# First feed-forward in parts of 8, 8 and 6 hidden tiles with six groups of gate and up pairs as seven block products, its state tables built behind them

## The chip, the cores and the metric

The kernel runs on one core of one Trainium2 chip. Times are device microseconds of that core. The engines are PE (TensorE: products), DVE (VectorE) and ACT (ScalarE) for work by element, POOL (GpSimd), and SP, which issues most of the transfers.

## What is computed

Two decoder layers over 528 tokens (16 meta tokens and 512) of 1024 features, in float32. The feed-forward has 2816 hidden features, 22 tiles of 128.

```python
def swiglu(x, w_gate, w_up, w_down):
    return (jax.nn.silu(x @ w_gate) * (x @ w_up)) @ w_down

def hybrid_layer(x, ...):
    x = layer_norm(ALPHA * x + 0.5 * swiglu(x, ffn1_w_gate, ffn1_w_up, ffn1_w_down), ln1_g, ln1_b)
    proj = x @ w_in
    ...                                   # three mixers: attention, short convolution, S5 scan
    x = layer_norm(ALPHA * x + mixed @ w_o, ln2_g, ln2_b)
    x = layer_norm(ALPHA * x + 0.5 * swiglu(x, ffn2_w_gate, ffn2_w_up, ffn2_w_down), ln3_g, ln3_b)
    return x
```

The S5 mixer needs tables made of its parameters alone: powers of its complex transition applied to the input weights (s_in_states, here in_step), to the output weights (s_out, here out_step), the powers themselves by token group (s_turns, here turn_step), and short kernels made of two of them (s_kernels).

## The kernel before

**Products.** Every product is made in three passes over parts that TensorE takes in its fast float32 form: high part of the weights by high part of the inputs, high by low, low by high (`product`). The 528 tokens are two halves of 264 columns, so a chunk of weights (8 tiles of 128x128) makes 48 products. A chunk is loaded by SP into one of two raw buffers (`load`), rounded to w_hi by ACT (`round_ahead`, `round_at`, line 1348), its remainder w_lo is made by POOL (`split`, line 642), and it lies in a ring of four slots until PE is done with it. PE, ACT, DVE and POOL each run an order written out by hand, and wait for each other on semaphores.

**Feed-forward.** The hidden tiles are made in three parts (PARTS: 6, 8, 8 tiles). In a part each tile needs a gate product and an up product; ACT takes the silu of the gate (hid_rest), DVE multiplies (line 1956) and splits the result (lines 1957 and 1958). Behind a part stand eight down products, one for each tile of 128 output features, which DVE takes into ln_in (line 1977; line 2108 in the second feed-forward). The down products of the last part are made in halves from the fifth on (`last_tiles`, line 840) so that the layer norm can begin on the first half; DVE takes them at line 1861 and goes on with the statistics (`tail`), and the products behind the norm (`first_products`, line 753 and 730) run over the first half of the tokens first.

**Crossed groups.** In the second feed-forward a pair of gate tiles, or of up tiles, is a 2x2 block product: the features in two halves, the tokens in two halves. It is made as seven products of blocks instead of eight (`crossed`, line 864). It needs turned inputs, that is four sums and differences of the blocks of x (DVE lines 1994 to 1997), rounded by ACT (turned_hi) with remainders by DVE (line 2002), made once per feed-forward; four sums of weight blocks per unit (`add_weights`, line 2018); and five additions of the results (`combine`, line 2036). The weights are loaded as pairs (w_pair). In most units ACT first copies three weight blocks into PSUM banks (`copy_block`), and the sums read them there. A crossed unit's seven forms (half chunks of 512 columns) are rounded and split one by one; form 5 waits for the second addition. In part 0 the second feed-forward has one plain pair and two pairs with only the gate crossed, in parts 1 and 2 gate and up are crossed.

**First feed-forward.** All its pairs are plain, and POOL, ACT, PE and SP run them in loops. DVE makes the state's tables beside them (`tables_beside`): angles, turn, coefficients beside the first three tiles; in_step beside part 0's later tiles and part 1's; out_step beside part 1's; turn steps 0 to 5 beside part 0's down products, 6 and 7 in part 1. PE transposes the tables beside part 1's down products (`turn_inputs`), and makes the kernels before part 2 (`s5_kernels`); ACT takes them (`take_turned`, `take_kernels`). Behind the layer norm come the mixer's first ten projections (`m1`), in which PE makes the states (line 1025) that DVE takes in `scan_begin` (line 2290).

## Time and profile before

| | us |
| --- | --- |
| median of 3 runs | 2550.42 (2549.15 to 2551.89) |
| the profiled execution | 2552.9 |
| its span | 2551.1 |
| PE busy in the span | 2509.9 |
| DVE busy | 1382.7 |
| ACT busy | 951.4 |
| POOL busy | 1230.0 |

The profile is one execution. Its page gives for each engine the busy time, a slice view, the chain of work that ended last, and the costliest groups of instructions. In a row of a timeline stand the start and the length in us, engine, line, operation, what it writes and reads, the number of instructions that the row merges, and in brackets how long the engine was idle before and what ended that. Layer 0's first feed-forward is from 10 to 406 us, its second from 918 to 1284; layer 1's first is from 1287 to 1682.

### The profile page before, as it was taken

To read this page: it belongs to the slowest core of one execution; us is meant where nothing else is said; L and a number is where in the kernel's file an instruction comes from. 1 tells how busy PE (TensorE), PEld (TensorE's weight loads), DVE (VectorE), ACT (ScalarE), POOL (GpSimd) and SP (SyncE) were. 2 spreads that over 40 slices of the span, in tenths; PEclk is the share of its full clock that TensorE was granted. 3 is DMA by queue.
4 is the path that set the end of the run, shared out by engine and by line. 5 is a ranking of instruction groups with operands and counts; after the bars stand their busy time and mean duration, and the time that the engine had idled before them with its cause. 6 is when DMAs were issued, how large, how long until landed. Compare 5 with 4: busy or idle time off the path is not lost.

```text
span 2551.1 us, 50807 instructions
## 1 busy us (share of the span) xinstructions
PE 2509.9 (98%) x20068; PEld 2391.4 (94%) x20068; DVE 1382.7 (54%) x2456; ACT 951.4 (37%) x1670; POOL 1230.0 (48%) x710
## 2 busy tenths in 40 slices
PE   9999999999999999999999999999999999999997
PEld 9999999998899999999999999999977788989897
DVE  6683134784453484535566841347844535835366
ACT  4222223235532243636452222232355322537363
POOL 4443344523234456867554443445332454668582
PEclk9999999999999999999999999999999999999999
DMA  5333233432223333333333323334322333324232
GB/s 154 93 91 90 84 91 84 111 82 65 60 79 89 95 92 100 91 108 89 95 93 99 90 83 91 91 83 110 84 65 63 87 88 106 100 83 117 83 102 81
DMA packets 479725, 232.25 MB, mean 91 GB/s; under 512 B 58960, under 2 KB 479056, under 8 KB 479536
## 3 DMA queue, kind: packets, MB, share of 16 engines
q1 hardware_dynamic: 460288, 220.53, 31.9%
q10 hardware_dynamic: 19248, 9.08, 1.5%
q8 instruction: 133, 2.18, 0.4%
q14 instruction: 56, 0.46, 0.1%
HBM read 220.79 MB, written 4.26 MB: 88 GB/s over the span
## 4 chain that ended last, share of the span: by engine, by line
PE 91%; DVE 4%; issue 3%; POOL 1%; ACT 1%; DMA 0%; ACTq 0%; POOLq 0%; DVEq 0%; SPq 0%
PE ps L730 64%; PE ps L864 14%; PE ps L840 4%; PE ps L753 3%; PE ps L1177 1%; PE ps L1216 1%; POOL w_lo L642 1%; PE ps L1181 1%; PE ps L1192 1%; DVE ln_in L1916 0%; PE ps L1099 0%; ACT ln_in L1348 0%; DVE ps L1933 0%; PE ps L1089 0%; PE ps L799 0%
## 5 line engine op out<-in xcount | busy, mean ns | idle before, releaser
L642 POOL TENSOR_TENSOR w_lo<-w_raw,w_hi 128x1024 fp32r<-128x1024 f32 (+4 forms) x400 | 850.5, 2133 | 1100.6 <-ACT w_hi L1348 1099.9
L1348 ACT ACTIVATE w_hi<-w_raw 128x1024 fp32r<-128x1024 f32 (+4 forms) x400 | 373.0, 936 | 659.3 <-PE ps L730 381.5
L730 PE MATMUL ps<-x_hi,w_hi 128*128 128x264 f32 (+2 forms) x2720 | 398.4, 296 | 2.5 <-issue 1.3
L730 PE MATMUL ps<-x_hi,w_lo 128*128 128x264 f32 (+2 forms) x2720 | 389.2, 293 | 0.6 <-POOL w_lo L642 0.6
L730 PE MATMUL ps<-x_lo,w_hi 128*128 128x264 f32 (+2 forms) x2720 | 389.0, 293 | 0.0
L730 PEld LDWEIGHTS ps<-x_hi,w_hi 128*128 128x128 f32 x2720 | 356.7, 189 | 16.7 <-issue 2.2
L730 PEld LDWEIGHTS ps<-x_hi,w_lo 128*128 128x128 f32 x2720 | 355.3, 188 | 11.0 <-POOL w_lo L642 1.3
L730 PEld LDWEIGHTS ps<-x_lo,w_hi 128*128 128x128 f32 x2720 | 355.4, 188 | 9.8
L1956 DVE TENSOR_TENSOR ps<-hid_rest,ps 128x528 f32<-128x528 f32 (+1 forms) x56 | 39.7, 710 | 242.8 <-PE ps L730 230.1
L730 PE MATMUL ps<-hid_hi,w_hi 128*128 128x264 f32 (+1 forms) x1008 | 158.2, 301 | 0.1
L730 PE MATMUL ps<-hid_hi,w_lo 128*128 128x264 f32 (+1 forms) x1008 | 156.6, 299 | 0.0
L642 POOL TENSOR_TENSOR w_lo<-w_sum,w_hi 128x512 fp32r<-128x512 f32 x90 | 118.7, 1325 | 78.3 <-ACT w_hi L1348 77.8
L730 PE MATMUL ps<-hid_lo,w_hi 128*128 128x264 f32 (+1 forms) x1008 | 156.4, 299 | 0.0
L642 POOL TENSOR_TENSOR w_lo<-w_pair,w_hi 128x512 fp32r<-128x512 f32 x108 | 145.1, 1358 | 9.7 <-ACT w_hi L1348 9.7
L730 PEld LDWEIGHTS ps<-hid_hi,w_hi 128*128 128x128 f32 x1008 | 137.1, 188 | 6.7 <-DVE ln_in L1977 0.6
L730 PEld LDWEIGHTS ps<-hid_hi,w_lo 128*128 128x128 f32 x1008 | 137.2, 188 | 6.3
L730 PEld LDWEIGHTS ps<-hid_lo,w_hi 128*128 128x128 f32 x1008 | 137.0, 188 | 6.2
L1348 ACT ACTIVATE hid_rest<-ps 128x528 f32 (+2 forms) x88 | 51.1, 603 | 173.9 <-PE ps L730 158.9
L2461 DVE SCALAR_TENSOR_TENSOR stat<-stat,ps 128x528 f32<-128x528 f32 (+1 forms) x32 | 22.2, 695 | 158.0 <-PE ps L730 158.0
L1348 ACT ACTIVATE w_hi<-w_sum 128x512 fp32r<-128x512 f32 x90 | 56.4, 631 | 101.6 <-DVE w_sum L2018 66.8
L864 PE MATMUL ps<-turned_lo,w_hi 128*128 128x264 f32 (+1 forms) x576 | 92.6, 283 | 0.0
L864 PE MATMUL ps<-turned_hi,w_hi 128*128 128x264 f32 (+1 forms) x576 | 92.5, 282 | 0.0
(349 smaller groups left out, 4303.3 us busy)
## 6 DMA issues: line engine op xcount, KB each, us to landing
w_raw<-in_w_in SPq DMA_DIRECT2D x82, 512.0 KB, 3.9
w_raw<-in_ffn_w_down SPq DMA_DIRECT2D x64, 512.0 KB, 3.9
w_raw<-in_ffn_w_up SPq DMA_DIRECT2D x56, 512.0 KB, 3.8
w_raw<-in_ffn_w_gate SPq DMA_DIRECT2D x48, 512.0 KB, 3.8
w_pair<-in_ffn_w_gate SPq DMA_DIRECT2D x40, 512.0 KB, 5.1
w_pair<-in_ffn_w_up SPq DMA_DIRECT2D x32, 512.0 KB, 5.2
w_raw<-in_ffn_w_down SPq DMA_DIRECT2D x32, 384.0 KB, 3.4
w_raw<-in_w_o SPq DMA_DIRECT2D x16, 512.0 KB, 3.9
```

Of the source, the lines that this page charges most:

```text
L642: pool.tensor_tensor(held(w_lo, c), src, held(w_hi, c).bitcast(f32), ALU.subtract).then_inc(w_split, 1)
L730: ins = nc.tensor.matmul(dst, wk, x[:, k0 + k, tokens], start=first and k == 0 and n == 0, stop=last and k == n_tiles - 1 and n == 2)
L753: ins = nc.tensor.matmul(dst, held(w, c + j, k * P, (k + 1) * P), x[:, k, tokens], start=k == 0 and n == 0, stop=k == nk - 1 and n == 2)
L840: ins = nc.tensor.matmul(ps[:, bank, 0:sp.half], held(w, c + d, k * P, (k + 1) * P), x[:, k, sp.halves[h]], start=p == 0 and k == 0, stop= ...
L864: ins = nc.tensor.matmul(ps[:, banks + bank, 0:sp.half], held(w, c + n, k * P, (k + 1) * P), x[:, k], start=start and i == 0 and k == 0, s ...
L1177: ins = nc.tensor.matmul(ps[0:nq, j % 2, 0:q0 + nq], qT[:, b, q0:q0 + nq], kT[:, b, 0:q0 + nq], start=True, stop=True)
L1181: ins = nc.tensor.matmul(ps[0:nq, h, 0:HALF], qT[:, b, q0:q0 + nq], kT[:, b, h * HALF:(h + 1) * HALF], start=True, stop=True)
L1192: nc.tensor.transpose(ps[:, 2 + buf, k * P:(k + 1) * P], pr[:, buf, k * P:(k + 1) * P], ident[:])
L1216: ins = nc.tensor.matmul(ps[64 * part:64 * part + 64, o_bank(i, b, part), q0 - first:end - first], vb[0:nk, b, k, :], PT[0:nk, k, q0:end], ...
L1348: return nc.scalar.activation(out, in_, f, **kw)
L1956: st.done(tt(up, gate, up, MUL))
L2461: ins = stt(two(stat[:, 2, sp.all]), two(stat[:, n % 2, sp.all]), 1.0, pair(2 * (n % 2) + 1, sp), ADD, MUL)
```

## The change

The first feed-forward gets parts of 8, 8 and 6 hidden tiles. Pairs 0 and 1 of part 0 stay plain; pairs 2 and 3 of part 0 and all four pairs of part 1 become crossed groups, gate and up, by the code of the second feed-forward, which is made general for both (w is 0 or 1). The three pairs of part 2 stay plain. There are 30 units per layer for 18. The turned inputs of the first feed-forward are made from ln_in at its start. Four of its forms skip half a slot of the ring.

The space of the turned inputs, of the weight pairs and of their sums is that of the tables. So in_step goes to the down products of part 1, behind a wait for the last unit's splits; out_step goes to the tiles of part 2; the turn steps go behind the layer norm, ahead of `scan_begin`. The load of s_out goes behind the third down product of part 1, on ACT's queue. PE's transposes go into pairs 1 and 2 of part 2, the kernels into the last tile of part 2 (banks 0 and 1), and PE waits for ACT's copies of them ahead of the down products. s_params moves by one row. The loops of the first feed-forward are written out. The second feed-forward stays as it is.

```diff
-TURN_WITH = [(0,), (1,), (2,), (3,), (4,), (5,), (6, 7), ()]
+TURN_BANK = [0, 1, 0, 1, 4, 5, 4, 5]
+OUT_STEPS = [(1, 2), (3, 4), (5, 6), (7,), (), ()]
+TAKE_WITH = {(0, 0): (), (0, 1): (), (1, 0): (0, 1), (1, 1): (2, 3, 4, 5), (2, 0): (6, 7), (2, 1): ()}
-PARTS = [(0, 6), (6, 8), (14, 8)]
+PARTS_OF = [[(0, 8), (8, 8), (16, 6)], [(0, 6), (6, 8), (14, 8)]]
+LAST = 2
+FIRST_CROSSED = 2
...
+def crossed_in(w, part, q):
+
+    if w:
+        return () if (part, q) == (0, 0) else (0, 1) if part else (0,)
+    return () if part == LAST or (part == 0 and q < FIRST_CROSSED) else (0, 1)
...
+BESIDE = [n for n, (w, part, q, what) in enumerate(UNITS)
+          if len(crossed_in(w, part, q)) == 2 and (what or (w, part, q - 1, 1) in UNITS)]
+SKIP_HALF = [UNIT_AT[0, 1, q, what] + 3 for q in (0, 2) for what in range(2)]
...
@@ SP
+            def load_pair(l, n):
+
+                w, part, q, what = UNITS[n]
...
+                if n in (FFN2_UNIT, FFN2_UNIT + 1):
+                    wait_apart(sp, chunk_done, done_at(l, B_WO + KD - 1))
+                elif g >= 2:
+                    wait_apart(sp, w_split, unit_split(g - 2))
...
+                            if part == 0 and crossed_in(w, part, q + 1):
+                                load_pair(l, UNITS.index((w, part, q + 1, 0)))
...
+                        for what in whats:
+                            n = UNITS.index((w, part, q, what))
+                            if n + 1 < N_CROSS and UNITS[n + 1][0] == w:
+                                load_pair(l, n + 1)
...
@@ PE
+            def regular_group(l, part, q, n0, t0, turned):
+
+                for j in range(2):
+                    c = GROUPS_AT[0, part, q] + 2 * j
+                    rounded(l, c)
+                    pe.wait_ge(silu_done, n0 + q * 2 + (j + 1))
+                    if turned and q == 2:
+                        pe.wait_ge(lf_taken, l * 8 + (4, 8)[j])
+                    product(pair(2 * j), c, 0, xh, xl, KD, True, True, split=(l, c)).then_inc(chunk_done, 1)
+                    if turned and (q, j) == (1, 1):
+                        turn_inputs(l, 2)
+                        turn_inputs(l, 3)
+                    if turned and (q, j) == (2, 0):
+                        turn_inputs(l, 6)
+                        turn_inputs(l, 7)
+                    if turned and (q, j) == (2, 1):
+                        pe.wait_ge(silu_done, n0 + (2 * q + 3))
+                        s5_kernels(l)
+                    rounded(l, c + 1)
+                    if part:
                         pe.wait_ge(z_taken, t0 + 2)
...
+                    if turned and q == 1:
+                        pe.wait_ge(silu_done, n0 + (2 * q + j + 3))
+                        turn_inputs(l, 4 * j)
+                        turn_inputs(l, 4 * j + 1)
...
                     pe.wait_ge(silu_done, n0 + (nf + 1))
+                    if w == 0 and part == LAST:
+                        pe.wait_ge(k_taken, l * 4 + 4)
...
@@ ACT
+                def first_group():
+
+                    c = GROUPS_AT[w, 0, 0]
...
+                    act.wait_ge(chunk_done, done_at(l, c))
+                    silu(0, pair(0, sp), 1.0)
+                    round_at(l, c + 1)
+                    if w == 0:
+                        act.wait_ge(s5p_in, l * 16 + 16)
+                        ACTV(s5p[:, 2], s5p[:, 2], ACT.Exp).then_inc(dt_done, 1)
+                    act.wait_ge(chunk_done, done_at(l, c + 2))
+                    silu(1, pair(2, sp), 1.0)
+                    round_at(l, c + 2)
+                    if w == 0:
+                        act.wait_ge(trig_in, l + 1)
+                        ACTV(s5p[:, 3], s5p[:, 3], ACT.Exp)
+                        ACTV(s5p[:, 6], s5p[:, 4], ACT.Sin)
+                        ACTV(s5p[:, 7], s5p[:, 4], ACT.Sin, scale=0.5).then_inc(trig_done, 1)
+                        act.wait_ge(par_in, l * 16 + 16)
+                        round_turned(0)
+                        round_turned(1)
+                    round_turned(2)
+                    round_turned(3)
+                    round_at(l, c + 3)
...
+                            if w == 0 and part == 1 and d == 2:
+                                wait_apart(act, w_split, unit_split(l * N_CROSS + FFN2_UNIT - 1))
...
+                                    act.dma_start(cl[r, :, :, 0].rearrange("p k q h -> p (k q) h"),
...
@@ DVE
+                def first_groups():
+
+                    c = GROUPS_AT[w, 0, 0]
+                    turn_inputs()
...
+                    s5_angles(l, st)
+                    hidden(0, 0, c + 1, 1)
+                    hidden(0, 1, c + 3, 3)
+                    s5_turn(l, st)
+                    for k in range(4):
+                        turned_rest(k)
+                    add_weights(0)
+                    hidden(0, 2, c + 5, 1)
+                    s5_coefficients(l, st)
+                    hidden(0, 3, c + 7, 3)
+
+                def regular_group(part, q):
+
+                    for j in range(2):
+                        hidden(part, 2 * q + j, GROUPS_AT[0, part, q] + (2 * j + 1), 2 * j + 1)
+                        for k in OUT_STEPS[2 * q + j]:
+                            out_step(l, k, st)
+                        if 2 * q + j == PARTS_OF[0][part][1] - 2:
+                            layer_norm_shift(sp)
...
                     for d in range(KD):
                         dve.wait_ge(chunk_done, done_at(l, bd + d))
                         ins = stt(two(z[:, d, sp.all]), pair(d % 2, sp), 0.5 / ALPHA, two(z[:, d, sp.all]), MUL, ADD)
                         follow(ins, z_taken, t0 + (d + 3))
+                        if w == 0 and part == 1:
+                            if d == 0:
+                                dve.wait_ge(w_split, unit_split(l * N_CROSS + FFN2_UNIT - 1))
+                            in_step(l, d, st)
...
-                ffn(l, B_FFN1, 0, st)
+                ffn(l, 0, st)
+                for d in range(8):
+                    turn_step(l, d, st)
                 scan_begin(l, st)
```

## Rows read from the trace of the kernel before

**Rows 1.** The page: engines; chain that ended last; costliest groups (busy, mean ns, idle).
```profile
PE 2509.9 (98%) x20068; PEld 2391.4 (94%) x20068; DVE 1382.7 (54%) x2456; ACT 951.4 (37%) x1670; POOL 1230.0 (48%) x710
...
PE 91%; DVE 4%; issue 3%; POOL 1%; ACT 1%; DMA 0%; ACTq 0%; POOLq 0%; DVEq 0%; SPq 0%
...
L1956 DVE TENSOR_TENSOR ps<-hid_rest,ps 128x528 f32<-128x528 f32 (+1 forms) x56 | 39.7, 710 | 242.8 <-PE ps L730 230.1
```

**Rows 2.** Stretches: length, busy of PE, PEld, DVE, ACT, POOL, clock, DMA.
```profile
146.88:170.08 23.20, 23.20 (x194) 23.20 (x194) 22.57 (x32) 5.24 (x7) 9.89 (x4) 1.00 0.31 89
...
1056.81:1077.20 20.39, 20.39 (x170) 20.39 (x170) 12.49 (x22) 14.16 (x28) 17.69 (x15) 1.00 0.38 105
```

**Rows 3.** Timelines at the start, layer 0 then layer 1; last ACT's turned_hi (min/median/max).
```profile
36.08 2.09 PE L730 MATMUL ps<-x_hi,w_hi 128*128 128x264 f32 x16
...
37.47 0.17 DVE L2140 TENSOR_SCALAR s_params<-s_params 128x16 f32<-128x16 f32 x1
...
1313.74 2.09 PE L730 MATMUL ps<-x_hi,w_hi 128*128 128x264 f32 x16
...
1317.87 0.17 DVE L2140 TENSOR_SCALAR s_params<-s_params 128x16 f32<-128x16 f32 x1
...
1319.61 1.28 ACT L1348 ACT_TABLE_LOAD   x1
...
1324.05 1.06 ACT L1348 ACTIVATE w_hi<-w_raw 128x1024 fp32r<-128x1024 f32 x1
...
L1348 ACT ACTIVATE turned_hi<-turned_raw x8: 1044/1067/1087, 939.6 to 2209.8; 128x1056 fp32r<-128x1056 f32 x4, 128x1024 fp32r<-128x1024 f32 x4
```

**Rows 4.** DVE, second feed-forward, layer 0: timeline of its entry; groups of one later group.
```profile
943.90 1.26 DVE L2002 SCALAR_TENSOR_TENSOR turned_lo<-turned_raw,turned_hi 128x1056 fp32r<-128x1056 f32 x1
...
945.80 2.78 DVE L2018 TENSOR_TENSOR w_sum<-w_sum,w_pair 128x512 f32<-128x512 f32 x1
...
956.82 2.24 DVE L2002 SCALAR_TENSOR_TENSOR turned_lo<-turned_raw,turned_hi 128x1056 fp32r<-128x1056 f32 x1
...
L2036 DVE TENSOR_TENSOR ps<-crossed_sum,ps 128x264 f32<-128x264 f32 x6 | 2.6, 437 | 2.5 <-PE ps L864 2.4
L2018 DVE TENSOR_TENSOR w_sum<-w_pair,ps 128x512 f32<-128x512 f32 x3 | 2.1, 686 | 2.8 <-ACT ps L1348 2.8
```

**Rows 5.** Timelines of POOL and DVE, layer 1, first feed-forward.
```profile
1312.09 4.88 POOL L642 TENSOR_TENSOR w_lo<-w_raw,w_hi 128x1024 fp32r<-128x1024 f32 x2 [5.33 <-ACT w_hi L1348]
...
1314.63 2.36 DVE L2136 TENSOR_SCALAR s_params<-s_params 128x16 f32<-128x16 f32 x1
```

**Rows 6.** POOL by shape, 947.95 to 961.45, entry of layer 0's second feed-forward.
```profile
L642 POOL TENSOR_TENSOR w_lo<-w_pair,w_hi 128x512 fp32r<-128x512 f32 x3 | 6.3, 2117 | 0.0
L642 POOL TENSOR_TENSOR w_lo<-w_sum,w_hi 128x512 fp32r<-128x512 f32 x4 | 5.9, 1484 | 1.4 <-ACT w_hi L1348 1.4
```

**Rows 7.** DVE's takes of down products of a part with 8 tiles.
```profile
1142.08 0.71 DVE L2108 SCALAR_TENSOR_TENSOR ln_in<-ps,ln_in 128x528 f32<-128x528 f32 x1 [5.11 <-PE ps L730]
1147.88 0.71 DVE L2108 SCALAR_TENSOR_TENSOR ln_in<-ps,ln_in 128x528 f32<-128x528 f32 x1 [5.09 <-PE ps L730]
```

**Rows 8.** PE behind the last part of layer 0's first feed-forward.
```profile
407.94 0.36 PE L753 MATMUL ps<-x_hi,w_hi 128*128 128x264 f32 x1 [1.84 <-DVE ln_in L1861]
```

**Rows 9.** DVE's tables: in_step's and out_step's rows; stretches of one in_step, the first.
```profile
166.40 1.93 DVE L2193 TENSOR_TENSOR s_tmp<-s_lambda,s_in_states 128x256 f32<-128x256 f32 x1
...
171.32 3.63 DVE L2244 TENSOR_TENSOR s_tmp<-s_lambda,s_out 128x256 f32<-128x256 f32 x4
...
166.48:171.29 4.81, 4.81 (x42) 4.81 (x41) 4.77 (x7) 1.21 (x2) 1.33 (x1) 1.00 0.38 109
61.77:68.81 7.04, 7.04 (x60) 7.04 (x59) 6.93 (x12) 2.98 (x4) 2.92 (x2) 1.00 0.19 56
```

**Rows 10.** Sum of three stretches with the turn steps; DVE's next work behind the norm.
```profile
sum 29.82, PE 29.82 PEld 29.82 DVE 26.00 ACT 7.37 POOL 12.98; mean PE 9.94 PEld 9.94 DVE 8.67 ACT 2.46 POOL 4.33
...
458.59 0.43 DVE L2290 TENSOR_TENSOR s_state<-ps,s_turns_re 128x260 f32<-128x260 f32 x1 [30.73 <-PE ps L1025]
```

More of the change, by code:

```diff
@@ L680, in _ @@
             for l in range(DEPTH):
-                ffn(l, B_FFN1)
+                for c in range(B_FFN1 + SLOTS, B_M1):
+                    split(l, c)
                 norm(l, 0, B_M1)
@@ new lines, in regular_group @@
+                def regular_group(part, q):
+                    for j in range(2):
+                        c = GROUPS_AT[0, part, q] + 2 * j
+                        round_at(l, c)
+                        act.wait_ge(chunk_done, done_at(l, c))
+                        silu(2 * q + j, pair(2 * j), 1.0)
+                        round_at(l, c + 1)
+                        if part == LAST:
+                            for n in TAKE_WITH[q, j]:
+                                take_turned(l, n)
+                    if part == LAST and q == 2:
+                        take_kernels(l)
```

472 lines of the change are left out of this document (184 added, 288 removed).

## Prediction

> **What bounds the kernel now.** I read the views in this order. The page [rows 1]: PE is busy for 98% of the span, and 91% of the chain that ended last is PE. So a change is worth the PE time that it takes away, less what it makes PE wait. Then the table of stretches [rows 2]: a group of the first feed-forward (two gate and two up tiles, 528 tokens) lasts 23.20 us with PE busy in all of it; a crossed group of the second feed-forward of layer 0, over the same 528 tokens, lasts 20.39 us and PE is busy in all of that too. That is 168 products for 192 at the same 0.121 us each, at a granted clock of 1.00. Then the timelines of each engine at the places where something moves: they give durations, and which wait ends last.
>
> **The groups that become products of blocks.** Twelve change, six per layer: pairs 2 and 3 of part 0 and the four of part 1. Each replaces 23.2 us by 20.4 [rows 2]: 12 x 2.8 = 33.6 us less. ACT, DVE and POOL must keep up; in the second feed-forward they do, busy for 14.2, 12.5 and 17.7 us of 20.4 [rows 2]. Spans, block copies and order are the same in the first, and its tables are built elsewhere, so nothing is added beside these groups. The new split into parts costs PE nothing by itself: 22 hidden tiles times 8 outputs either way.
>
> **Entry: the turned inputs,** new in the first feed-forward of both layers. I price two waits, by the rows of layer 1 [rows 3].
> ACT first. It now rounds the four turned inputs (1.07 us each) before the weights of gate tile 3. The angles are ready at 1318.0; three table loads with the exponential and the sines took 4.4 us (1319.6 to 1324.0), so they end at 1322.5, the roundings at 1326.8, the weight chunk (1.06) at 1327.8. PE starts pair 1 at 1313.7 and wants the chunk 11.6 us later, at 1325.3: it waits 2.5 us. In layer 0 the angles are ready 1.6 us after the start of pair 1 instead of 4.3: chunk at 47.4, wanted at 47.7, no wait.
> DVE next. From the angles on it does hidden tiles 0 and 1 (2 x 3 instructions of 0.71 [rows 1]), the turn (some 17 of 0.16), four remainders of turned inputs (1.26), four sums of weights (0.69), hidden 2, the coefficients (some 20 of 0.16) and hidden 3 [rows 3 to 5]: 4.3 + 2.7 + 5.0 + 2.8 + 2.1 + 3.2 + 2.1 = 22.2 us, to 1340.3. At the entry of the second feed-forward, 943.90 to 959.06, the same remainders and sums with one hidden tile took 15.2 us for 10.0 unhindered, because single instructions were drawn out to 2.24 and 2.78 us [rows 4]. Those 5.2 us make it 1345.5. ACT's copy of a weight block waits for hidden 3, whose bank it takes, and behind it on ACT stand the roundings of forms 5 and 6; copy, one sum (0.69) and two combinations (0.43 each) add 2.2 us [rows 4]: 1347.7. PE, 2.5 us late, wants form 5 at 1346.7. So 1.0 us is lost; unhindered nothing is, with twice the hindrance 6.2. I take 2.0, near the low end, since its row is of the same instructions. In layer 0 both sides lie 2.5 to 2.7 us earlier: 2.0 again. Entry: 2.5 + 2.0 + 2.0 = 6.5 us, bounds 2.5 and 14.9.
> What draws DVE out is to be seen in [rows 5]: a tiny instruction lasts 2.36 us and ends with the POOL splits that ran from 1312.09 to 1316.97. The Trainium skill ("SBUF — State Buffer", section "SBUF: two separate sides") says that VectorE and GpSimd take a shared pair of ports as an exclusive lock, for instance for a VectorE instruction with two SBUF inputs. By that rule the remainders and sums hold up POOL as well, which speaks against this change; the trace agrees, as the seven forms of that entry took 12.2 us [rows 6].
>
> **Exit: a shorter last part.** It falls from 8 to 6 hidden tiles, so less PE work lies beside the layer norm: a down product takes 4.35 us for 5.80 [rows 7], a half 2.2 for 2.9. Before, PE waits 1.84 us for a DVE take (L1861) ahead of the mixer's first products [rows 8]. After the first half's sums three halves are left to PE, 2.1 us shorter in future, while DVE's chain to that take shrinks by 0.7 only, a wait for one of the halves. So the gap becomes some 3.2 to 3.4 us: +1.6 a layer, 3.2 in all, bounds 0 and 4.4 (no part of 2.2 hidden).
>
> **The state's tables, moved.** In_step goes beside the down products of part 1. One took 4.8 us, of which its first instruction 1.93; the first, with two complex products, 6.9 [rows 9]. With the take (0.71) the cycle is 5.5 us for a product of 5.80 [rows 7]. The first runs over by 1.9, but PE asks only for the take of two products earlier: 3.3 us of slack remain, nothing is lost. Out_steps take at most 4.5 us [rows 9]; two and a hidden tile are 11.1 of the 11.6 us of a tile, and the table is ready some 10 us before the kernels' products ask. Transposes and kernels' products stay PE work, the same number, between other products; ACT's copies of the kernels lie beside the last up product. The load of s_out moves to ACT's queue behind the third down product of part 1, with over 30 us to land, and ACT is mostly idle there. On SP pair loads stand ahead of down weights and wait for the split of two units back, as in the second feed-forward. The Toeplitz copies wait for the kernels some 90 us longer and still lie ahead of the end of the mixer's projections.
> The turn steps go behind the layer norm: the stretches with them hold 26.0 us of DVE work, less five takes of 0.71: 22.5 us. DVE is idle for 30.73 us ahead of 458.59, where PE's states come [rows 10]: hidden, 8 us to spare; without that cover 22.5 us per layer.
>
> **The rivals.** (1) *The edges cost nothing beyond ACT's wait*: -33.6 + 2.5 = -31.1. For it: the second feed-forward's entry has the drawn-out instructions and no PE gap. Against: one hidden tile there, no tables. (2) *The tables push the down products.* If a second hindrance of 1.3 us (1.93 against some 0.65) falls into each in_step, the cycle is 6.8 us; 8 x 1.0 less the slack of 3.3 is 4.7 us per layer: -23.9 + 9.4 = -14.5. With three it is 8 x 2.3 - 3.3 = 15.1 per layer: +6, no gain. For it: POOL splits beside these products; against: one split per 5.8 us, as beside the gates, where [rows 9] shows one hindrance. (3) *POOL sets the pace, and it is slower than before.* A group then lasts 14 splits; the seven at the entry of the second feed-forward took 1.75 us each [rows 6], which makes 24.5 us: 12 x (24.5 - 23.2) + 9.7 = +25 us. It decides at 23.2 / 14 = 1.66 us a split (1.60 with the edges). For it: POOL has but 2.7 us spare; against: 17.7 / 14 = 1.26 us in settled groups [rows 2]. The skill's lock is this mechanism; by that rule alone a group lies between 20.4 and 24.5 us. (4) *It doesn't do what it says*: groups are crossed but PE runs slower in unrolled code or waits for pair loads. At 21.5 us a group it is 12 x 1.7 = 20.4 less and 9.7 more: -10.7. Against: the crossed groups are unrolled already, without a gap [rows 2].
>
> **How the numbers follow.** Forecast: -33.6 + 6.5 + 3.2 = -23.9 us. The profiled execution took 2552.9 us (span 2551.1 and 1.8 around it), so 2529.0. The median of the runs is 2550.4, 2.5 lower: 2526.5 us. Chances: forecast 0.55 (2521 to 2532), free edges 0.20 (2519.3), late tables 0.14 (2536, of which 0.04 reach 2545 or more), POOL's pace 0.05 (2575), slower products 0.06 (2540). The bounds give -33.6 + 2.5 + 0 = -31.1 and -33.6 + 14.9 + 4.4 = -14.3: 2519.3 to 2536.1; I reach down to 2517, since ACT's wait may be absent too. 0.2%, 5.1 us, is about what a measurement of this kernel can tell from no change. Faster by more: 0.90; within: 0.05; slower: 0.05.
>
> **What would show it.** Silus of the first feed-forward some 20.4 us apart over six groups per layer and 23.2 over the others; PE gaps of 1 to 3 us at the first crossed group and at gate tile 3 of layer 1, ended by ACT roundings; some 3.3 us for 1.84 behind the last part; takes 5.8 us apart in part 1; turn steps ended before the states. It is wrong if POOL's splits take over 1.5 us in settled groups, if down products of part 1 lie over 6 us apart, or if PE waits for turn steps or a pair's load.

## The result, and the profile after

The changed kernel takes 2534.49 us (median of five runs, 2532.34 to 2539.03) against 2550.93 us of five runs of the kernel before beside them: a ratio of 0.9941, 95% interval 0.9929 to 0.9952, so 16.4 us less. The profiled execution took 2532.34 us with a span of 2530.5, the lowest of the five; its span is 20.6 us under that of the kernel before. A second set of five runs gave 2535.63 us (ratio 0.9937, 0.9923 to 0.9951), and its profile a span of 2533.8.

Line numbers have moved: products are L746, the first tiles behind a norm L769, crossed products L881, all of ACT's work L1376, POOL's splits L667, DVE's takes of down products L2136, its takes of halves L1879, and the six instructions of a complex product L2209 to L2216.

The page of the changed kernel, its line of engines and its chain that ended last (they answer to [rows 1]):

```profile
PE 2482.1 (98%) x19780; PEld 2361.1 (93%) x19780; DVE 1520.0 (60%) x2664; ACT 1047.4 (41%) x1900; POOL 1347.1 (53%) x830
...
PE 88%; DVE 5%; issue 4%; ACT 1%; POOL 1%; DMA 1%; ACTq 0%; POOLq 0%; SPq 0%; DVEq 0%
```

PE is busy 27.8 us less, with 288 products fewer, and the part of the chain that isn't PE has grown from 9% to 12%. So some of what was taken away came back as waits. Stretches (columns as in [rows 2]): a crossed group of part 1, two tiles of part 2, and the first step of in_step.

```profile
180.49:200.86 20.37, 20.37 (x170) 20.37 (x170) 12.49 (x22) 13.65 (x26) 17.58 (x15) 1.00 0.38 103
285.83:309.81 23.98, 23.48 (x194) 23.51 (x195) 21.90 (x33) 5.25 (x7) 10.08 (x4) 1.00 0.29 82
237.35:246.60 9.25, 9.25 (x78) 9.25 (x78) 9.11 (x13) 2.12 (x2) 5.02 (x3) 1.00 0.64 151
```

A crossed group lasts 20.37 us with PE busy in all of it: the gain is there, in full. Three places give some of it back. First, the entry. PE at the first crossed unit of layer 1, and then of layer 0:

```profile
1329.93 0.64 PE L881 MATMUL ps<-x_hi,w_lo 128*128 128x264 f32 x4
1333.88 1.06 PE L881 MATMUL ps<-turned_hi,w_hi 128*128 128x264 f32 x4 [3.31 <-issue]
1334.73 1.08 PE L881 MATMUL ps<-turned_lo,w_hi 128*128 128x264 f32 x4
...
1337.92 0.65 PE L881 MATMUL ps<-x_hi,w_lo 128*128 128x264 f32 x4
...
68.47 0.73 PE L881 MATMUL ps<-turned_hi,w_hi 128*128 128x264 f32 x4 [1.95 <-issue]
```

and DVE beside the first of them:

```profile
1309.88 6.82 DVE L2001 SCALAR_TENSOR_TENSOR turned_lo<-turned_raw,turned_hi 128x1056 fp32r<-128x1056 f32 x2
...
1322.83 1.32 DVE L2182 TENSOR_TENSOR s_params<-s_turn 128x16 f32<-128x16 f32 x1
...
1325.37 1.28 DVE L2186 TENSOR_TENSOR s_params<-s_params 128x16 f32<-128x16 f32 x1
...
1329.14 0.71 DVE L1974 TENSOR_TENSOR ps<-hid_rest,ps 128x528 f32<-128x528 f32 x1
...
1332.17 0.69 DVE L2017 TENSOR_TENSOR w_sum<-w_pair,ps 128x512 f32<-128x512 f32 x1 [0.83 <-ACT ps L1376]
1332.89 0.43 DVE L2035 TENSOR_TENSOR crossed_sum<-crossed_first,ps 128x264 f32<-128x264 f32 x1
1333.35 0.43 DVE L2035 TENSOR_TENSOR crossed_sum<-crossed_sum,ps 128x264 f32<-128x264 f32 x1
```

PE has made forms 0 to 4 of the unit (the row of 1329.93 ends form 4) and goes on at 1333.88, 0.10 us after the second addition (1333.35 + 0.43): form 5 waits for it. Layer 0 has one more gap there, of 0.38 us (77.82). "issue" names no releaser; the row of DVE does. The addition stands behind hidden tile 3 (from 1329.14), and that behind the coefficients, 1322.6 to 1329.1.

Second, beside part 1's down products. DVE, then POOL, then PE, in layer 1:

```profile
1531.99 0.71 DVE L2136 SCALAR_TENSOR_TENSOR ln_in<-ps,ln_in 128x528 f32<-128x528 f32 x1
...
1534.43 0.67 DVE L2212 TENSOR_TENSOR s_tmp<-s_lambda,s_in_states 128x256 f32<-128x256 f32 x1
1535.14 2.75 DVE L2215 TENSOR_TENSOR s_in_states<-s_tmp 128x256 f32<-128x256 f32 x1
1537.71 0.68 DVE L2216 TENSOR_TENSOR s_in_states<-s_tmp 128x256 f32<-128x256 f32 x1
1538.43 0.71 DVE L2136 SCALAR_TENSOR_TENSOR ln_in<-ps,ln_in 128x528 f32<-128x528 f32 x1
...
1533.63 3.74 POOL L667 TENSOR_TENSOR w_lo<-w_raw,w_hi 128x1024 fp32r<-128x1024 f32 x1 [2.68 <-ACT w_hi L1376]
...
1539.19 2.22 PE L746 MATMUL ps<-hid_hi,w_hi 128*128 128x264 f32 x16 [0.37 <-DVE ln_in L2136]
```

Takes lie 6.44 us apart (1531.99 to 1538.43) for a down product of 5.80 [rows 7], DVE has no idle time, and PE waits for the take. Of an in_step's six instructions one lasts 2.75 us and ends 0.52 us behind the split (1537.89 for 1533.63 + 3.74 = 1537.37), so it got its own 0.66 us of work done about when the split was over. PE has five such gaps in layer 0 (0.31, 0.32, 0.41, 0.39, 0.54 us) and four in layer 1 (0.30, 0.37, 0.43, 0.45).

Third, the exit, behind the first feed-forward of layer 0 (they answer to [rows 8]):

```profile
394.39 0.36 PE L769 MATMUL ps<-x_hi,w_hi 128*128 128x264 f32 x1 [1.13 <-DVE ln_in L1879]
...
397.42 0.36 PE L769 MATMUL ps<-x_hi,w_hi 128*128 128x264 f32 x1 [2.43 <-DVE ln_in L1879]
```

3.56 us for 1.84; layer 1 has 1.13 + 2.52. The two profiles differ also where the change does nothing, here to the good of the changed kernel: PE in the state's outputs, before and after.

```profile
537.72 0.56 PE L1099 MATMUL ps<-s_state,s_out 64*64 64x66 f32 x19 [1.87 <-issue]
```

```profile
523.23 0.57 PE L1127 MATMUL ps<-s_state,s_out 64*64 64x66 f32 x20 [0.40 <-issue]
```

Layer 0 of the kernel before also waited 1.30 us ahead of part 2 (264.65), beside ACT's copies of the kernels (from 262.87), which the change moved; layer 1 had no such gap.

### The profile page after: what moved, and what is told of

The parts are those of the page before. It is cut to its first block, busy times and chain, and to the rows that moved or that the text cites. A ratio compares the mean times of both kernels' runs of the same rounds, so it can differ in the third digit from the quotient of the medians.

```text
span 2530.5 us, 50304 instructions
## 1 busy us (share of the span) xinstructions
PE 2482.1 (98%) x19780; PEld 2361.1 (93%) x19780; DVE 1520.0 (60%) x2664; ACT 1047.4 (41%) x1900; POOL 1347.1 (53%) x830
## 4 chain that ended last, share of the span: by engine, by line
PE 88%; DVE 5%; issue 4%; ACT 1%; POOL 1%; DMA 1%; ACTq 0%; POOLq 0%; SPq 0%; DVEq 0%
PE ps L746 52%; PE ps L881 23%; PE ps L856 3%; PE ps L769 3%; PE ps L1205 1%; PE ps L1244 1%; POOL w_lo L667 1%; PE ps L1209 1%; PE ps L1220 1%; DVE s_in_states L2216 0%; ACT ln_in L1376 0%; DMA w_pair<-in_ffn_w_gate 0%; ACT x_hi L1376 0%; DVE ln_in L2136 0%; DVE s_tmp L2209 0%
## 5 line engine op out<-in xcount | busy, mean ns | idle before, releaser
L667 POOL TENSOR_TENSOR w_lo<-w_raw,w_hi 128x1024 fp32r<-128x1024 f32 (+3 forms) x352 | 753.1, 2149 | 895.6 <-ACT w_hi L1376 895.5
L1376 ACT ACTIVATE w_hi<-w_raw 128x1024 fp32r<-128x1024 f32 (+3 forms) x352 | 319.6, 913 | 589.2 <-PE ps L746 249.3
L746 PE MATMUL ps<-x_hi,w_hi 128*128 128x264 f32 (+2 forms) x1952 | 297.0, 301 | 2.2 <-issue 1.0
L746 PE MATMUL ps<-x_hi,w_lo 128*128 128x264 f32 (+2 forms) x1952 | 288.5, 297 | 0.6 <-POOL w_lo L667 0.6
L746 PE MATMUL ps<-x_lo,w_hi 128*128 128x264 f32 (+2 forms) x1952 | 288.4, 297 | 0.0
L746 PEld LDWEIGHTS ps<-x_hi,w_hi 128*128 128x128 f32 x1952 | 259.1, 188 | 16.9 <-issue 1.8
L746 PEld LDWEIGHTS ps<-x_hi,w_lo 128*128 128x128 f32 x1952 | 259.3, 188 | 11.1 <-POOL w_lo L667 1.3
L667 POOL TENSOR_TENSOR w_lo<-w_sum,w_hi 128x512 fp32r<-128x512 f32 x150 | 197.1, 1321 | 135.6 <-ACT w_hi L1376 134.8
L746 PEld LDWEIGHTS ps<-x_lo,w_hi 128*128 128x128 f32 x1952 | 259.4, 188 | 9.7
L667 POOL TENSOR_TENSOR w_lo<-w_pair,w_hi 128x512 fp32r<-128x512 f32 x180 | 238.7, 1341 | 23.6 <-ACT w_hi L1376 23.6
L746 PE MATMUL ps<-hid_hi,w_hi 128*128 128x264 f32 (+1 forms) x1040 | 162.3, 300 | 1.8 <-DVE ln_in L2136 1.7
L1376 ACT ACTIVATE w_hi<-w_sum 128x512 fp32r<-128x512 f32 x150 | 93.9, 630 | 166.6 <-DVE w_sum L2017 101.5
L746 PE MATMUL ps<-hid_hi,w_lo 128*128 128x264 f32 (+1 forms) x1040 | 161.1, 299 | 0.0
L746 PE MATMUL ps<-hid_lo,w_hi 128*128 128x264 f32 (+1 forms) x1040 | 161.0, 299 | 0.0
L881 PE MATMUL ps<-turned_hi,w_hi 128*128 128x264 f32 (+1 forms) x960 | 155.0, 283 | 5.3 <-issue 5.3
L2136 DVE SCALAR_TENSOR_TENSOR ln_in<-ps,ln_in 128x528 f32<-128x528 f32 (+1 forms) x64 | 45.0, 703 | 186.3 <-PE ps L746 185.7
L881 PE MATMUL ps<-turned_lo,w_hi 128*128 128x264 f32 (+1 forms) x960 | 155.3, 284 | 0.0
L881 PE MATMUL ps<-turned_hi,w_lo 128*128 128x264 f32 (+1 forms) x960 | 154.6, 283 | 0.0
L746 PEld LDWEIGHTS ps<-hid_hi,w_hi 128*128 128x128 f32 x1040 | 141.4, 188 | 9.7 <-DVE ln_in L2136 2.3
L746 PEld LDWEIGHTS ps<-hid_hi,w_lo 128*128 128x128 f32 x1040 | 141.3, 188 | 6.3
L746 PEld LDWEIGHTS ps<-hid_lo,w_hi 128*128 128x128 f32 x1040 | 141.1, 188 | 6.2
L881 PEld LDWEIGHTS ps<-turned_hi,w_hi 128*128 128x128 f32 x960 | 132.1, 188 | 6.4 <-issue 5.6
```

The costliest lines, as they stand in the source:

```text
L667: pool.tensor_tensor(held(w_lo, c), src, held(w_hi, c).bitcast(f32), ALU.subtract).then_inc(w_split, 1)
L746: ins = nc.tensor.matmul(dst, wk, x[:, k0 + k, tokens], start=first and k == 0 and n == 0, stop=last and k == n_tiles - 1 and n == 2)
L881: ins = nc.tensor.matmul(ps[:, banks + bank, 0:sp.half], held(wx, c + n, k * P, (k + 1) * P), x[:, k], start=start and i == 0 and k == 0, ...
L1376: return nc.scalar.activation(out, in_, f, **kw)
L2136: ins = stt(two(z[:, d, sp.all]), pair(d % 2, sp), 0.5 / ALPHA, two(z[:, d, sp.all]), MUL, ADD)
```

## The experiments

All medians stand against the kernel before run on the same chip, which gave 2549.9 to 2550.9 us. The changed kernel is 2534.5 and 2535.6 in its two sets.

**1. The coefficients out of the entry.** Nothing of the first feed-forward needs them.

```diff
                     hidden(0, 2, c + 5, 1)
-                    s5_coefficients(l, st)
                     hidden(0, 3, c + 7, 3)
...
                         follow(ins, z_taken, t0 + (d + 3))
+                        if (w, part, d) == (0, 0, 0):
+                            s5_coefficients(l, st)
```

> The changed kernel with the coefficients of the state (some 20 small instructions on DVE, 6.5 us in the trace of the changed kernel, 1322.6 to 1329.1) taken out from between hidden tiles 2 and 3 and put beside the first down product of part 0, where DVE is mostly idle. Theory A (DVE's chain hidden 3, block copy, sum, two additions ends PE's wait ahead of form 5): hidden 3 ends 6.5 us earlier, so the gaps of 1.95 us (layer 0) and 3.31 us (layer 1) go, and with them the slow stretch behind the second (four rows of 1.06 us for 0.65, 1.6 us): 6.8 us less, 2534.5 - 6.8 = 2527.7 us (2525.5 to 2530). Rival B (PE waits for forms whose roundings or splits are late, whatever DVE does): the gaps stay within 0.5 us, 2534 us. Rival C (the drawn-out remainders in front are what counts and a new wait for DVE's sums takes the place of the old one): half goes, 2531.

Measured: 2527.45 us (2525.43 to 2530.52), ratio 0.9914 (0.9900 to 0.9927). The gaps of 1.95, 0.38 and 3.31 us are gone, and the slow stretch too. DVE and then PE at the same place in layer 1:

```profile
1320.36 0.71 DVE L1976 TENSOR_TENSOR hid_lo<-ps,hid_hi 128x528 fp32r<-128x528 f32 x1
1322.71 0.69 DVE L2017 TENSOR_TENSOR w_sum<-w_pair,ps 128x512 f32<-128x512 f32 x1 [1.64 <-ACT ps L1376]
1323.43 0.43 DVE L2035 TENSOR_TENSOR crossed_sum<-crossed_first,ps 128x264 f32<-128x264 f32 x1
1324.67 0.43 DVE L2035 TENSOR_TENSOR crossed_sum<-crossed_sum,ps 128x264 f32<-128x264 f32 x1 [0.81 <-PE ps L881]
...
1325.38 0.64 PE L881 MATMUL ps<-x_hi,w_lo 128*128 128x264 f32 x4
1325.86 0.65 PE L881 MATMUL ps<-turned_hi,w_hi 128*128 128x264 f32 x4
```

Now DVE waits for PE ahead of the second addition (0.81 us), not PE for DVE. Theory A holds for the gaps, B and C fall. But the 7.0 us are not the entry alone. From the silu ahead of it to the last one of part 0 layer 0 is 2.85 and layer 1 5.05 us shorter, 7.9 in all. Beside part 0's down products, where the coefficients now stand, the two layers lose 0.8 us (a gap of 0.36 us at 117.95). And beside part 1's down products, which this edit doesn't touch, layer 0 lost nothing any more (2.75 us less than in the changed kernel), while layer 1 lost about what it had lost before. DVE and POOL there, layer 0:

```profile
247.97 0.71 DVE L2135 SCALAR_TENSOR_TENSOR ln_in<-ps,ln_in 128x528 f32<-128x528 f32 x1
248.71 2.01 DVE L2210 TENSOR_TENSOR s_tmp<-s_lambda,s_in_states 128x256 f32<-128x256 f32 x1
...
247.81 2.40 POOL L667 TENSOR_TENSOR w_lo<-w_raw,w_hi 128x1024 fp32r<-128x1024 f32 x1 [3.32 <-ACT w_hi L1376]
```

Here the split starts ahead of the take and is over 1.5 us after in_step's first instruction began. That instruction is drawn out by 1.35 us, the split by nothing, and the takes lie 5.56 to 5.87 us apart. The first step took 7.03 us. So the same in_step beside the same products has two courses, and this one is that of the prediction.

**2. in_step spread.** A pause beside the third down product, the last step behind the first hidden tile of part 2, out_steps one tile later.

```diff
-OUT_STEPS = [(1, 2), (3, 4), (5, 6), (7,), (), ()]
+OUT_STEPS = [(), (1, 2), (3, 4), (5, 6), (7,), ()]
+IN_STEPS = [(0,), (1,), (), (2,), (3,), (4,), (5,), (6,)]
...
+                        if (q, j) == (0, 0):
+                            in_step(l, 7, st)
...
-                            in_step(l, d, st)
+                            for k in IN_STEPS[d]:
+                                in_step(l, k, st)
```

> The changed kernel with in_step's eight steps spread otherwise: none beside the third down product of part 1, the last one behind the first hidden tile of part 2, and the out_steps one tile later each. Theory A (DVE's cycle of take and in_step, 6.45 us in the trace against a down product of 5.80, holds up the products): DVE catches up once in the middle, and the gaps ahead of the later down products (0.31 + 0.32 + 0.41 + 0.39 + 0.54 us in layer 0, 0.30 + 0.37 + 0.43 + 0.45 in layer 1, with 0.1 us of slower first products each) go: 3.5 to 4.4 us less, 2534.5 - 4 = 2530.5 us (2529 to 2532). Rival B (the gaps come with each down product for another reason, such as the slower splits of 3.9 us): they stay, 2534.5. Rival C (the out_steps, one tile later, are late for the kernels' products): PE waits there, 2536 or more.

Measured: 2529.76 us (2528.54 to 2531.01), ratio 0.9918 (0.9904 to 0.9932), 4.7 us under the changed kernel. Of the nine gaps two are left, ahead of the fourth down product, one in each layer:

```profile
254.43 1.69 PE L747 MATMUL ps<-hid_hi,w_hi 128*128 128x264 f32 x12 [0.33 <-DVE ln_in L2139]
...
1519.62 1.69 PE L747 MATMUL ps<-hid_hi,w_hi 128*128 128x264 f32 x12 [0.65 <-DVE ln_in L2139]
```

They are the debt of the first step, two complex products that took 9.25 us beside a product of 5.80. The pause does more than give slack: behind it the steps run as in layer 0 of experiment 1 (in layer 0 from 268.17 on the first instruction takes 2.05 to 2.22 us, and the splits 2.40). The out_steps, a tile later, were in time.

**3. Splits made thin.** What draws in_step out. The low parts of part 1's down weights are left out but for 8 of 1024 columns.

```diff
+                n = 8 if DOWN_AT[0][1] <= c < DOWN_AT[0][1] + KD else COLS[c % CH]
-                pool.tensor_tensor(held(w_lo, c), src, held(w_hi, c).bitcast(f32), ALU.subtract).then_inc(w_split, 1)
+                pool.tensor_tensor(held(w_lo, c, 0, n), src[:, 0:n], held(w_hi, c, 0, n).bitcast(f32),
+                                   ALU.subtract).then_inc(w_split, 1)
```

> The changed kernel with POOL's splits of part 1's down weights made over 8 of 1024 columns: the low parts of these weights are left out. Theory A (one instruction of each in_step is drawn out from 0.66 to 2.75 us because POOL's split holds it up): every instruction of in_step lasts some 0.66, the cycle of take and in_step is 6.45 - 2.1 = 4.35 us, takes lie 5.80 us apart and PE has no gap over 0.2 us beside these products; some 4 us less than the changed kernel, profiled 2528. Rival B (DVE's sixth instruction is long by its own addresses, s_in_states written with a stride): it stays 2.75 us and the gaps of 0.3 to 0.5 stay.

Measured in one execution: 2529.62 us. DVE and POOL in layer 0:

```profile
249.38 0.41 POOL L668 TENSOR_TENSOR w_lo<-w_raw,w_hi 128x8 fp32r<-128x8 f32 x1 [5.39 <-ACT w_hi L1378]
...
250.78 0.65 DVE L2214 TENSOR_TENSOR s_tmp<-s_lambda,s_in_states 128x256 f32<-128x256 f32 x1
251.47 0.66 DVE L2217 TENSOR_TENSOR s_in_states<-s_tmp 128x256 f32<-128x256 f32 x1
254.11 0.71 DVE L2138 SCALAR_TENSOR_TENSOR ln_in<-ps,ln_in 128x528 f32<-128x528 f32 x1 [1.48 <-PE ps L748]
```

The instruction of 2.75 us lasts 0.66, take and in_step together 4.32 us, DVE waits 1.48 us for PE in each cycle, and PE has no gap beside these products. From the last silu ahead of them to the first behind they take 61.34 us in both layers, for 64.09 and 63.62 in the changed kernel: 5.0 us in all are the price of the split's hold on DVE, as the two met in the changed kernel. Theory A holds. (Layer 0 of experiment 1 took 61.3 us too, with whole splits.)

**4. Part 0 plain.** Only the four groups of part 1 crossed.

```diff
-FIRST_CROSSED = 2
+FIRST_CROSSED = 4
...
-SKIP_HALF = [UNIT_AT[0, 1, q, what] + 3 for q in (0, 2) for what in range(2)]
+SKIP_HALF = []
...
```

The lines left out let DVE make hidden tiles 4 to 7 plain and move the load of the first pair of weights.

> The changed kernel with all of part 0 of the first feed-forward plain again; only the four pairs of part 1 are crossed (eight groups in all, for twelve). The turned inputs are still made at the start. By 2.8 us a group the four plain groups cost 11.2 us. Theory A (the entry's losses come only from crossing at once behind the first pairs: gaps of 1.95 and 0.38 in layer 0, of 3.31 and 0.37 in layer 1 and 1.6 us of slow clock): they go, 7.2 to 7.6 us come back, 2534.5 + 11.2 - 7.4 = 2538.3 us (2536.5 to 2540.5). Rival B (they come from making the turned inputs at the start, whoever uses them): they stay, 2545.7. Rival C (a crossed group of part 0 is worth less than 2.8 us): below 2535.

Measured: 2544.31 us (nine runs, 2541.02 to 2547.60), ratio 0.9976 (0.9966 to 0.9986). It is 6.0 us from A's number and 1.4 from B's, but the trace decides for A: no gap stands where the four were, though the turned inputs are made at the same place, so B falls. And a group is worth what it should be; a plain one of part 0 and a crossed one of part 1 in this kernel:

```profile
65.31:88.51 23.20, 23.20 (x194) 23.20 (x193) 8.13 (x19) 5.36 (x6) 10.28 (x5) 1.00 0.36 101
184.44:204.81 20.37, 20.37 (x170) 20.37 (x169) 12.50 (x22) 14.14 (x27) 17.68 (x15) 1.00 0.38 104
```

Of the 6 us over A's time 2.0 are found beside part 1's down products, where the same in_step met the splits at other moments (silu to silu 65.29 and 64.37 us for 64.09 and 63.62; its first step took 10.3 us, with instructions of 1.68, 2.50 and 2.75). The rest lies in stages that this edit doesn't touch, 1.6 us of it in one longer gap ahead of layer 1's second feed-forward; why it is longer was not found.

**5. Two edits together.** Experiments 1 and 2, with the pause one product earlier (`IN_STEPS = [(0,), (), (1,), (2,), (3,), (4,), (5,), (6,)]`), to pay the first step's debt where it arises.

> The two edits that paid, together: the state's coefficients beside the first down product of part 0, and in_step's steps with a pause beside the second down product of part 1 (one down product earlier than in the run before, because the first step took 9.3 us for two complex products and left a gap of 0.33 and 0.65 us at the fourth), the eighth behind the first hidden tile of part 2. Theory A (two separate waits, so the gains add): 7.0 + 4.7 us off 2534.5, and 1 us for the two gaps: 2521.8 us (2520 to 2524.5). Rival B (they share slack: what PE doesn't wait at the entry it waits for at the down products): 2525 or more.

Measured: 2521.62 us (2519.99 to 2523.14), ratio 0.9888 (0.9873 to 0.9903). The gains add, so B falls by its number. They are not two wholly separate waits, though: in layer 0 experiment 1 alone had already taken the loss beside part 1's down products. With both edits it is gone in both layers (61.3 us from silu to silu in either), and beside part 0's down products, with the coefficients, PE loses 1.1 and 0.7 us in the second set's profile. That set (expected as follows) gave 2521.31 us.

> The kernel with both edits again, beside the one with the takes in the other order: 2521.6 us (2520 to 2523).

**6. The exit: is it the shorter part?** Each half of the last four down products multiplies two of its six hidden tiles a second time, so that PE takes a part of 8's time there.

```diff
-                            for k in range(nk):
+                            order = [*range(nk), *((0, 1) if which == 0 else ())]
+                            for i, k in enumerate(order):
...
```

> The changed kernel in which each output half of the last four down products of the first feed-forward multiplies two of its six hidden tiles a second time, so that PE takes the time of a part of 8 tiles there (8 halves x 6 products x 0.121 us = 5.8 us more work a layer); what is computed differs in that. Theory A (the gap behind the first feed-forward went from 1.84 to 3.56 us because the shorter last part leaves PE less to do beside DVE's layer norm): the gap falls to about 1.8 us in each layer; 2535 + 11.6 - 3.5 = 2543 us. Rival B (the gap grew for another reason, such as DVE's tail being later by the tables): it stays 3.5 us, 2547 us.

Measured in one execution: 2541.60 us. The same row as in the changed kernel, layer 0 and layer 1:

```profile
402.55 0.36 PE L769 MATMUL ps<-x_hi,w_hi 128*128 128x264 f32 x1 [1.82 <-DVE ln_in L1880]
...
1672.77 0.36 PE L769 MATMUL ps<-x_hi,w_hi 128*128 128x264 f32 x1 [1.83 <-DVE ln_in L1880]
```

The gap is back at the 1.84 us of [rows 8]: DVE's tail is as long as it was, and PE had 5.8 us less to do beside it, of which 1.7 show as a wait. Theory A holds.

**7. DVE's last two takes together.** At every layer norm, on top of experiment 5; and once on the changed kernel alone.

```diff
-                        if h == 0 and k in (2, 3):
-                            st.done(add_half_square(k + 3, 1, k + 8))
-                            take_half(k + 4, 1)
+                        if h == 0 and k == 2:
+                            st.done(add_half_square(5, 1, 10))
+                            take_half(6, 1)
+                            take_half(7, 1)
+                        if h == 0 and k == 3:
+                            st.done(add_half_square(6, 1, 11))
```

> The run before, and at every layer norm DVE takes the last two output halves of the second half one right behind the other. In the trace PE has long made the last half (393.25) when DVE takes it at 396.84, behind a square, a scaling and a remainder, and PE's second column of the next products waits for its bank: gaps of 1.13 + 2.43 us behind the first feed-forward (1.84 before the change), 1.83, 2.79 and 1.93 behind the others. Theory A (the order of DVE's takes sets the gap): PE starts 2.4 us earlier and waits later for tiles of x, of which DVE makes one in 1.5 us where PE uses 0.7: 0.5 to 1.5 us less at each of five norms, some 4 us, 2518 us. Rival B (DVE's whole tail is the bound, the order changes nothing): the gaps split up and their sum stays, within 1.5 us of the run before. Rival C: the tiles of x come 0.9 us later for the two takes ahead of them, and each norm loses that: 4 us more.

> Only the order of DVE's takes at the layer norms changed, all else as the changed kernel: a look at where PE then waits. Theory A: one gap of about 1.1 us for the bank, then small ones of 0.3 to 1 us for tiles of x, 2.5 us in sum for 3.56 behind the first feed-forward; 2530.5 us. Rival B: the sum of the gaps stays 3.5 us, 2534 us. Rival C: over 4 us in sum, 2538.

> The kernel with both edits and DVE's takes in the other order again. In the look at the changed kernel with this order the gaps behind the first feed-forward were 2.3 us for 3.6 and fell apart in three; in the timed runs it was 0.9 us below the kernel with both edits, within their spread. If the order brings what the gaps show (1.3 us each behind the two first feed-forwards, 0.3 to 0.5 behind the others), 2518.5 us, 3 us below the run beside it; if PE's first products are then slower by the same time, no difference, within 1 us.

Measured: on top of experiment 5 first 2520.74 us (2518.36 to 2523.47), within the spread of the run beside it (2521.62), then 2517.17 us (2516.38 to 2518.20) beside 2521.31. On the changed kernel alone one execution gave 2530.34. The first pair left it open; the second speaks for a gain, of 4.1 us, and over both sets it is 1 to 4. PE behind layer 0's first feed-forward in the last of them:

```profile
389.21 0.36 PE L770 MATMUL ps<-x_hi,w_hi 128*128 128x264 f32 x1 [1.14 <-DVE ln_in L1880]
...
391.81 0.39 PE L770 MATMUL ps<-x_hi,w_hi 128*128 128x264 f32 x1 [0.44 <-DVE x_lo L1958]
...
393.55 0.39 PE L770 MATMUL ps<-x_hi,w_hi 128*128 128x264 f32 x1 [0.73 <-DVE x_lo L1958]
```

One wait of 2.43 us for a bank became short ones for tiles of x (there is one more of 0.23 between them): the sum fell from 3.56 to 2.54 us. Behind the five layer norms that have products behind them, PE's waits of 0.25 us and more sum to 10.5 us in this profile, for 13.7 without this edit. The kernels differ also in the clock behind these gaps. A stretch behind layer 0's second feed-forward without this edit (from the end of its gap), and one with it (from the start of the first wait):

```profile
1266.05:1273.91 7.86, 7.86 (x46) 7.86 (x47) 5.46 (x14) 4.88 (x11) 2.38 (x1) 0.62 0.44 130
```

```profile
1264.60:1272.60 8.00, 5.54 (x43) 4.88 (x43) 5.93 (x16) 5.56 (x13) 2.38 (x1) 1.00 0.45 131
```

Behind one gap of 2.79 us PE ran at a granted clock of 0.62 for 7.9 us, so that gap and 46 products took 10.65 us; with the wait cut into short ones, none over 1.0 us, it stayed at 1.00, and waits and 43 products took 8.00. But that is one execution of each. The other profile of the kernel without this edit, and the other one with it, show the opposite at the same place:

```profile
1266.69:1274.55 7.86, 6.86 (x56) 6.44 (x57) 5.70 (x16) 4.89 (x11) 2.65 (x2) 1.00 0.45 133
```

```profile
1268.00:1278.40 10.40, 9.99 (x49) 9.69 (x50) 3.36 (x11) 2.95 (x7) 1.42 (x2) 0.53 0.17 50
```

The first stands behind one gap of 2.78 us, at full clock; the second behind short waits of 0.44, 1.00 and 0.51 us, at 0.53 for 10.4 us. So the length of the wait doesn't settle the clock. What speaks for the edit is the mean granted clock of whole executions: 0.9965 over the eight with it (0.995 to 0.997) for 0.9945 over the eight without (0.993 to 0.996). That is 5 us of 2518 at most, an estimate with half the speed lost wherever the clock was low. Shorter waits and a higher clock can each account for the gain; they were not told apart. This kernel, 2517.17 us at a ratio of 0.9870 (0.9854 to 0.9887), is the fastest of all.

**8. The changed kernel again.**

> The changed kernel itself once more, beside the runs of this call, since its five runs lay 6.7 us apart (2532.3 to 2539.0) and the profiled one was the lowest. If its profile was a lucky one, a second profile shows more gaps or more slow clock by some 2 us, and the median is again 2534.5 (2533.5 to 2536).

Measured: 2535.63 us (2530.28 to 2538.80). The second profile has the entry's and the exit's gaps of over 1 us again, within 0.2 us. Beside part 1's down products it has four and six gaps for five and four, and the two layers lose 6.1 us there for 5.0. PE and its clock behind the gap in layer 0's entry are:

```profile
68.73 0.73 PE L881 MATMUL ps<-turned_hi,w_hi 128*128 128x264 f32 x4 [2.10 <-issue]
```

```profile
68.73:73.33 4.60, 4.60 (x26) 4.60 (x26) 2.87 (x5) 3.99 (x8) 4.60 (x5) 0.64 0.73 207
```

In the first profile the stretch behind the 1.95 us gap was at 1.00. So the same wait costs 1.5 us more in some executions. In the five runs of the first set time goes with the mean granted clock: 0.994 in the fastest (2532.34), 0.991 in the slowest (2539.03). By the estimate of experiment 7 that is 7.6 us at most, for a spread of 6.7.

## Why the prediction came out as it did

The sign held, and two thirds of the gain came (16.4 us for 23.9). The time lay 8 us above the forecast, inside the whole range, but outside the 2521 to 2532 us given to the forecast itself. It is 1.5 us from the 2536 of rival 2, the late tables, which had a chance of 0.14. The prediction's own sign of being wrong showed as well: takes beside part 1's down products lay 6.44 us apart. Of the four terms the groups' and the exit's held as worked out, the entry's by luck, and the tables' failed. The terms, in us:

| term | predicted | measured | by |
| --- | --- | --- | --- |
| twelve groups | -33.6 | -34.0 (12 x 2.83) | stretches; 23.20 and 20.37 in experiment 4 |
| entry | +6.5 | +7.2 | the trace has 1.95 + 0.38 + 3.31, and 1.55 of slow clock; experiment 1 took back 7.9 there |
| exit | +3.2 | +3.5 | trace; cause by experiment 6 |
| tables beside down products | 0 | +4.7 to +5.0 | experiments 2 and 3 (6.1 in the second profile) |
| sum | -23.9 | -18.3 to -18.6 | |

The medians give -16.4 (-14.8 with the second set of the changed kernel, against 2550.4), the two profiles -20.6. In the profiles the kernel before had 1.87 and 1.30 us of gaps for 0.40 and none in the changed one; the first comes and goes with the execution (none there in the second profile). The remaining 2 to 4 us between sum and medians have no place of their own in the traces, but the granted clock has room for them. Its mean over the runs is 0.9928 and 0.9926 in the two sets of the changed kernel and 0.9950 and 0.9958 in the kernel before beside them. That is 5.6 and 8.1 us more, at most and as an estimate (half the speed lost at low clock), of which the table counts 1.55. The prediction had no term for the clock.

*The tables: the step that failed.* "The cycle is 5.5 us for a product of 5.80" rested on an in_step of 4.8 us beside plain gates [rows 9], with one hindrance of some 1.3 us. In the changed kernel it takes 5.7 beside down products (6.44 less the take): unhindered 3.6 (experiment 3), and the hindrance is 2.1. The rows tell why. In_step is under way when the split starts (1533.63), and two more of its instructions start and go through, at 0.67 us each. The split lasts 3.74 us for 2.40, so it seems to have waited 1.34 us, until 1534.97, and then held the next instruction until its end: nearly a whole split. In layer 0 of experiment 1 the split started 0.9 us ahead of in_step, under the take, and held DVE for the rest only. There the hindrance was 1.35 us, the first step took 7.03 us for the 6.9 predicted, and nothing was lost, as predicted. So the prediction priced the mild course and took it for the only one. The mechanism was on the list as rival 2, with the wrong count: not a second hindrance but a longer one in each step. The first step, put at 6.9 us, took 9.25, with two hindrances (9.65 in layer 1). Such a first step went before the long course wherever no pause followed it, but it isn't needed: with the takes in the other order on the changed kernel (experiment 7), layer 0's first step took 4.9 us, and PE had three gaps of 0.48 to 0.54 us later. What brings the long course on was not found.

With the sizes of the long course the prediction's own working gives the loss: 9.25 + 0.71 - 5.80 = 4.2 us for the first step and 5 x 0.65 for the steps whose take a product still waits for, less 5.1 us that a take may be late [rows 7], is 2.3 us a layer; measured were 2.3 and 2.75. The bound to take was the split's own length, and not the one row of another place.

*The entry: the sum right by luck, its parts not.* ACT's wait of 2.5 us in layer 1 did not come. I set the angles 4.3 us behind the start of pair 1, as in layer 1 before [rows 3]; they came 0.6 us behind it (they were ready at 1300.55, and the pair began at 1299.96). Of these 3.7 us 1.2 are one of DVE's tiny instructions, held up for 2.36 us before [rows 5] and for 1.15 now; the rest was not traced. Gate tile 3's chunk was rounded by 1308.9 for a PE that came at 1311.6. DVE's chain was the right one, down to the block copy that waits for hidden tile 3, but it was more drawn out: from the first remainder (1307.54) to the second addition (1333.78) it took 26.2 us for 17.4 unhindered, 8.8 us of hindrance and waiting for my 5.2, and the coefficients alone 6.5 for 3.2. And I had no term for the clock: 16 products behind the gap took 3.49 us for 1.94, at a granted clock of 0.53, next to the lower of its two levels (1.2 for 2.4 GHz). That a missing wait, a longer chain and a term left out come to 7.2 us for 6.5 is luck.

*The exit* was worked out as it came: 1.7 us a layer for 1.6, and experiment 6 turned it back. The clock behind it is low in both kernels (0.58 over the 4.1 us from 407.94 before, 0.60 from 398 to 402 after), so it adds nothing to the difference there.

*The turn steps* were hidden as forecast. They ran from 413.7 to 433.5 in layer 0 (19.8 us for my 22.5), and DVE then waited:

```profile
448.08 0.43 DVE L2306 TENSOR_TENSOR s_state<-ps,s_turns_re 128x260 f32<-128x260 f32 x1 [13.78 <-PE ps L1054]
```

*Out_steps, transposes, kernels, the load of s_out* cost PE nothing beyond their own products; in layer 1 the kernels' products took 2.5 us for 2.0.

*The rivals.* (1) free edges: no, by experiments 1 and 6. (2) late tables: yes, in this measure. (3) POOL's pace: no; the splits of a settled group took 17.58 us of 20.37. Of the Trainium skill's lock ("SBUF — State Buffer", section "SBUF: two separate sides") the trace of the changed kernel shows both sides: DVE's instruction with two SBUF inputs waits for the split (2.75 us for 0.66), and the split beside such instructions is longer (3.74 us, and 2.40 at 293.54 beside a hidden tile). The same page of the Trainium skill (section "Who interferes with whom") says that a DVE instruction with at most one SBUF input doesn't contend with GpSimd, outside the 2-port perf modes. The take, which reads a bank and one SBUF tensor, agrees: it lasts 0.69 to 0.71 us in all 64 instances of the profile. (4) slower products: no; 20.37.

## What to carry to other kernels

Where small work by element is moved beside short products, count its cycle with one instruction of it drawn out by nearly a whole instruction of the engine beside it (here POOL's split), not by what the old place showed; if cycle and product lie within a tenth of each other, leave a pause in every few. The pause gives slack, and here it also brought back the milder course. Work that nothing near it needs (here the coefficients) doesn't belong into the chain ahead of the first user of a new scheme: moving it gave 7.9 us there and cost 0.8 elsewhere. When an edit pays, look at the places it doesn't touch too: 2.75 us more of experiment 1's gain came from one. And a wait of 2 to 3 us on PE can cost half as much again in clock, but not in each execution, so judge such waits by several, and by the mean clock of all runs.

## What the runs showed of the hardware

- One split of 128x1024 on POOL draws out one DVE instruction of the complex products by 2.1 us (0.66 to 2.75), and is drawn out by DVE in turn (2.40 to 3.74 us). With the split cut to 8 columns both go (experiment 3). When they meet decides: with the split started under the take, the instruction is drawn out by 1.2 to 1.5 us only and the split not at all (experiment 1, layer 0). The same first step took 7.03 us in one kernel, 9.25 in another and 10.3 in a third.
- An instruction with a single SBUF input can be drawn out as well; on DVE in layer 0's entry, while POOL split from 57.59 to 61.41:

```profile
60.23 1.21 DVE L2187 TENSOR_SCALAR s_params<-s_params 128x16 f32<-128x16 f32 x1
61.47 0.18 DVE L2188 TENSOR_TENSOR s_turn<-s_turn,s_params 128x16 f32<-128x16 f32 x1
```

- A gap of 1.95 us on PE was followed by full clock in one execution and one of 2.10 by a clock of 0.64 over 4.6 us in another. Behind gaps of 2.8 and 3.3 us it was 0.62 and 0.53, but 1.00 behind one of 2.78, and behind one of 1.84 us in the kernel before 0.58 over 4.1 us. Behind short waits up to 1.00 us it was 1.00 in one execution and 0.53 in another. In the changed kernel such a stretch cost 1.5 to 1.6 us behind the entry's gaps.
